# Gate products one tile of 128 outputs at a time, over the steps and the ends of all attention stages

## The reference

```python
# first block, per layer (D = 1024, 256 tokens)
h = rms_norm(x, mix_norm_g[l]);  proj = h @ w_in[l]
sb_q, sb_k, sb_v, sw_q, sw_k, sw_v, gate_logits = split(proj)     # gate_logits: 2 x 1024
y_sb  = stick_breaking_attention(sb_q, sb_k, sb_v) @ w_branch_sb[l]       # 8 heads of 64
y_swa = sliding_window_sink_attention(rope(norm(sw_q)), rope(norm(sw_k)), sw_v, sinks) @ w_branch_swa[l]
gates = sigmoid(gate_logits)
x = x + (gates[0] * y_sb + gates[1] * y_swa) @ w_out[l]
x = x + square(relu(rms_norm(x, mlp_norm_g[l]) @ w_up[l])) @ w_down[l]
# second block, per layer
x = layer_norm(a * x + 0.5 * swiglu(x))
#   token mixing: one w_in product, then four branches, each with a gate of 1024 outputs (4 x 1024):
#   ya gated MLP over tokens, yb short convolution, yc latent attention (MLA, 8 heads of 96),
#   yd sparse attention (compressed, selected and window keys, 8 heads of 64)
#   mix = (g0 * ya + g1 * yb + g2 * yc + g3 * yd) @ w_o[l]
x = layer_norm(a * x + mix);  x = layer_norm(a * x + cross_attention(x, mem))
x = layer_norm(a * x + 0.5 * swiglu(x))
```

## Time and profile before

| | us |
|---|---|
| median of 3 runs (2394.44 to 2394.92) | 2394.6 |
| the profiled execution | 2392.54 |
| its span, first to last instruction | 2390.8 |
| TensorE busy in the span | 2311.5 |
| VectorE busy | 1353.6 |
| ScalarE busy | 1152.1 |
| POOL busy | 186.9 |
| mean granted TensorE clock | 0.99 of full speed |
| read from memory | 392.9 MB, 165 GB/s over the span |

### The profile page before, as it was taken

How to read it: one execution, slowest core, us unless ns; L and a number is a source line. 1 busy time by engine, 2 the same in 40 slices (tenths; PEclk the granted TensorE clock), 3 DMA queues, 4 the chain that set the end, 5 groups by cost and what they waited for, 6 DMA issues and landing times.

```text
span 2390.8 us, 38487 instructions
## 1 busy us (share of the span) xinstructions
PE 2311.5 (97%) x16084; PEld 2123.2 (89%) x16098; DVE 1353.6 (57%) x1782; ACT 1152.1 (48%) x1797; POOL 186.9 (8%) x191
## 2 busy tenths in 40 slices
PE   7999999999999999999999999999999999998998
PEld 6988988888998998799998889989988999897997
DVE  4556555646664545655566665465555555776454
ACT  4754544674553444545443544454444445355443
POOL 0001210001110210000003001111100000110110
PEclk9999999999999999999999999999999999999999
DMA  6324555432555655554533545565555444263554
GB/s 223 132 97 152 184 197 181 163 121 97 190 189 185 222 182 189 171 181 141 168 106 110 190 156 181 191 208 188 187 174 184 155 158 143 80 205 134 184 178 146
DMA packets 109005, 395.93 MB, mean 166 GB/s; under 512 B 12374, under 2 KB 12544, under 8 KB 108576
## 3 DMA queue, kind: packets, MB, share of 16 engines
q1 hardware_dynamic: 104400, 377.53, 47.7%
q0 software_dynamic: 4432, 15.93, 2.2%
HBM read 392.92 MB, written 1.05 MB: 165 GB/s over the span
## 4 chain that ended last, share of the span: by engine, by line
PE 89%; DVE 5%; ACT 3%; DMA 1%; issue 1%; SPq 0%; DVEq 0%; ACTq 0%
PE psum L390 80%; PE psum L805 2%; PE psum L771 2%; DVE w_low L347 2%; PE psum L707 2%; DMA ring<-in_weights 1%; PE psum L789 1%; ACT w_high L344 1%; ACT attn_p L887 1%; PE psum L1773 1%; DVE mx L831 1%; DVE xT_low L666 0%; PE psum L1113 0%; ACT xT_high L660 0%; PE psum L1101 0%
## 5 line engine op out<-in xcount | busy, mean ns | idle before, releaser
L347 DVE TENSOR_TENSOR w_low<-ring,w_high 128x1024 fp32r<-128x1024 f32 x704 | 863.5, 1255 | 577.3 <-ACT w_high L344 575.7
L344 ACT ACTIVATE w_high<-ring 128x1024 fp32r<-128x1024 f32 x704 | 718.0, 1052 | 302.1 <-DMA ring<-in_weights 301.5
L390 PE MATMUL psum<-xT_high,w_high 128*128 128x256 f32 x2976 | 848.0, 285 | 0.0
L390 PE MATMUL psum<-xT_low,w_high 128*128 128x256 f32 x2976 | 843.3, 283 | 0.0
L390 PE MATMUL psum<-xT_high,w_low 128*128 128x256 f32 x2976 | 843.2, 283 | 0.0
L390 PEld LDWEIGHTS psum<-xT_high,w_high 128*128 128x128 f32 x2976 | 572.6, 192 | 0.8
L390 PEld LDWEIGHTS psum<-xT_low,w_high 128*128 128x128 f32 x2976 | 572.6, 192 | 0.4
L390 PEld LDWEIGHTS psum<-xT_high,w_low 128*128 128x128 f32 x2976 | 572.3, 192 | 0.0
L390 PE MATMUL psum<-w_high,hidden 128*128 128x512 f32 x1216 | 376.6, 390 | 0.0
L390 PEld LDWEIGHTS psum<-w_high,hidden 128*128 128x128 f32 x1216 | 228.3, 188 | 47.1
L390 PE MATMUL psum<-w_low,hidden 128*128 128x512 f32 x608 | 236.6, 389 | 0.0
(11 more groups left out here) (233 smaller groups left out, 2196.0 us busy)
## 6 DMA issues: line engine op xcount, KB each, us to landing
ring<-in_weights SPq DMA_DIRECT2D x706, 512.0 KB, 3.7
pages<-in_affine POOLq DMA_DIRECT2D x16, 512.0 KB, 5.6
ring<-in_weights SPq DMA_DIRECT2D x8, 440.0 KB, 3.3
pages<-in_gains POOLq DMA_DIRECT2D x4, 512.0 KB, 5.1
pages<-in_mem POOLq DMA_DIRECT2D x2, 1024.0 KB, 6.1
ring<-in_weights SPq DMA_DIRECT2D x4, 384.0 KB, 3.1
x<-in_x_in SPq DMA_DIRECT2D x2, 512.0 KB, 4.3
pages<-in_rows POOLq DMA_DIRECT2D x2, 512.0 KB, 6.2
```

The lines of the kernel that those rows point to most:

```text
L344: eng.activation(high, raw, ACT.Copy).then_inc(self.flag("w_rounded").sem, 1)
L347: eng.tensor_tensor(self.w_low[:, piece % SLOTS, 0:width], raw, high.bitcast(F32), ALU.subtract).then_inc(self.flag("w_split").sem, 1)
L390: m = pe.matmul(out, a, b, start=(first and i == 0), stop=(last and i == len(pairs) - 1))
```

## The change

Each gate tile of 128 outputs becomes a group of its own, 16 per layer in the first block and 32 in the second. It has its own bank (half filled), its own tanh of 128 x 256 and its own piece to split behind it; before, a group was two tiles, in the first block with one tanh of 128 x 512, in the second with two of 128 x 256. Matmuls, weight pieces and their bytes are the same. The tiles are distributed anew:

- first block: step 0 of the scan has tiles 0 and 1, steps 1 to 8 one each (2 to 9); 10 lies before the wait for the copied output, 11 before the turn of the keys; 12 beside step 1 and 13 beside step 6 of the sliding window, 14 behind its last values, 15 between the turn of its output and the wait for the parts;
- second block: 0 before the product `uq` and its wait for the turned latents; 1 and 2, 3 and 4, 5 and 6 where the groups 0, 1, 2 were; MLA's steps 0, 1, 2 and 6 have two each, 3, 4, 5 one; 18 behind MLA's values; 19 and 20, 21 and 22 around the compression; 23 to 31 beside steps 0 to 8 of the sparse attentions, then `ya` and `yb` at steps 9 to 16; `yc` 0 and 1 lie before the wait for the last output, 2 and 3 behind its turn.

The order of the weight pieces in memory, the counts of the semaphores and the bank order follow.

```diff
-GATES_PRE, GATES_MLA, GATES_NSA = 3, 10, 12
+GATES_SB = [[0, 1], [2], [3], [4], [5], [6], [7], [8], [9]]
+BESIDE_SWA = {0: [("ysb", 1)], 1: [("gate", 12)], 2: [("ysb", 2)], 4: [("ysb", 3)], 6: [("gate", 13)]}
+GATES_MLA = 19
+BESIDE_MLA = {0: [7, 8], 1: [9, 10], 2: [11, 12], 3: [13], 4: [14], 5: [15], 6: [16, 17]}
+BESIDE_NSA = dict(enumerate([("gate", n) for n in range(23, 32)] + [(y, n) for y in ("ya", "yb") for n in range(4)]))
...
@@ first block, TensorE
+            def gate(n):
+                c.gemm_features(pe, l, stream, banks, "gate", ("gate", n), xTf, KD, [("gate", n)])
...
                 if 1 <= h <= 8:
                     later_keys(h - 1)
-                if h < 8:
-                    c.gemm_features(pe, l, stream, banks, "gate", ("gate", h), xTf, KD,
-                                    [("gate", 2 * h), ("gate", 2 * h + 1)])
+                if h < 9:
+                    for n in GATES_SB[h]:
+                        gate(n)
                 if h >= 2:
                     sb_values(h - 2)
+            gate(10)
             pe.wait_ge(*c.flag("osb_ready").at(l, 2))
...
+            gate(11)
             c.wait_read_out(pe, l, "osb0", "osb1")
...
+            c.attend_tensor(pe, l, ("swa",), lambda i: [gate(n) if key == "gate" else branch_sb(n)
+                                                        for key, n in BESIDE_SWA.get(i, [])])
+            gate(14)
             pe.wait_ge(*c.flag("o_drained").at(l, 2))
...
+            gate(15)
             c.wait_read_out(pe, l, "osw0", "osw1")
@@ first block, ScalarE (VectorE splits the same pieces in the same places)
+            def gate(n):
+                act.activation(gates[:, n, :], c.filled(act, l, banks, ("gate", n))[:, 0:SEQ], ACT.Tanh, scale=0.5
+                               ).then_inc(*c.drained(banks, ("gate", n)))
+                after(("gate", n))
...
+            gate(14)
             for i in range(2):
                 c.part_out(act, l, "act", f"osw{i}", 4 + i, *(x[:, 2 * i:2 * i + 2, :] for x in oswT))
+            gate(15)
@@ second block, TensorE
+            c.gemm_features(pe, l, stream, banks, "gate", ("gate", 0), xT, KD, [("gate", 0)])
             c.wait_read_out(pe, l, "lat0", "lat1")
...
-            c.attend_tensor(pe, l, ("mla",), lambda i: group(BESIDE_MLA[i]) if i in BESIDE_MLA else None)
+            c.attend_tensor(pe, l, ("mla",), lambda i: gates(*BESIDE_MLA.get(i, [])))
+            gates(18)
...
             c.attend_tensor(pe, l, nsa, lambda i: group(BESIDE_NSA[i]) if i in BESIDE_NSA else None)
+            for n in range(2):
+                group(("yc", n))
             pe.wait_ge(*c.flag("o_drained").at(l, 8))
             turn_features("od", lambda k, t: o[:, t, k * P:(k + 1) * P])
-            group(("yc", 3))
+            for n in range(2, 4):
+                group(("yc", n))
             c.wait_read_out(pe, l, "od0", "od1")
```

More of the change, by code:

```diff
@@ L98, in stream_1, with gates, branch @@
     s.matrix("sbk", "w_in", D, span(512, 512), P, split=True)
-    s.matrix("gate", "w_in", D, span(2304, 2048), P, split=True)
-    s.matrix("ysb", "w_branch_sb", 512, span(0, D), P, split=True)
+    def gates(first, end):
+        for n in range(first, end):
+            for k in range(KD):
+                s.add(("gate", n, k), "w_in", k * P, span(2304 + n * P, P), split=True)
+    def branch(first, end):
+        for n in range(first, end):
+            for k in range(4):
+                s.add(("ysb", n, k), "w_branch_sb", k * P, span(n * P, P), split=True)
+    gates(0, 12)
+    branch(0, 4)
+    gates(12, 13)
+    branch(4, 8)
+    gates(13, 16)
     s.matrix("ysw", "w_branch_swa", 512, span(0, D), P, split=True)
@@ L121, in gates @@
             def gates(first, end):
-                for n in range(first, end):
-                    for tile in (2 * n, 2 * n + 1):
-                        for k in range(KD):
-                            s.add(("gate", tile, k), "w_in_2", k * P, span(4280 + tile * P, P), split=True)
+                for tile in range(first, end):
+                    for k in range(KD):
+                        s.add(("gate", tile, k), "w_in_2", k * P, span(4280 + tile * P, P), split=True)
+            gates(0, 1)
             s.matrix("uq", "mla_wuq_2", 256, span(0, 768), 384)
@@ L1001, in block_1 @@
             banks.add((key, t))
-    for key, n in (("sbq", 2), ("sbk", 2), ("gate", 8), ("ysb", 4), ("ysw", 4)):
-        for n in range(n):
+    for key, first, end in (("sbq", 0, 2), ("sbk", 0, 2), ("gate", 0, 12), ("ysb", 0, 2), ("gate", 12, 13), ("ysb", 2, 4),
+                            ("gate", 13, 16), ("ysw", 0, 4)):
+        for n in range(first, end):
             banks.add((key, n))
@@ L1048, in block_1 @@
     c.unit_list([window])
-    BESIDE = {0: 1, 2: 2, 4: 3}
     def added(t, n):
@@ L1401, in _ @@
                                          ).then_inc(*c.flag("sb_kept").one())
-                after(("gate", h))
+                for n in GATES_SB[h]:
+                    after(("gate", n))
                 next(side, None)
@@ L1405, in _ @@
                 pass
+            after(("gate", 9))
             c.settle(dve, l, "dve_step")
@@ L1409, in _ @@
                 dve.tensor_copy(osb[:, t, :], c.psum[:, 6 + t, :]).then_inc(*c.flag("osb_ready").one())
+            after(("gate", 10))
             for i in range(2):
@@ L1414, in _ @@
                             ).then_inc(*c.read_out("dve", "swq0"))
+            after(("gate", 11))
             c.turned(dve, l, "swk")
@@ L1564, in block_2 @@
             banks.add((key, t))
-    for key, n in (("gate", 16), ("ya", 4), ("yb", 4), ("yc", 4), ("yd", 4)):
-        for i in range(n):
+    for key, n in (("gate", 32), ("ya", 4), ("yb", 4), ("yc", 4), ("yd", 4)):
+        for i in range(1 if key == "gate" else 0, n):
             banks.add((key, i))
@@ L1994, in _ @@
             c.attend_scalar(act, l, nsa, beside_nsa)
+            for n in range(2):
+                after(("yc", n))
             for i in range(2):
                 c.part_out(act, l, "act", f"od{i}", 4 + i, *(x[:, 2 * i:2 * i + 2, :] for x in od_parts))
-            after(("yc", 3))
+            for n in range(2, 4):
+                after(("yc", n))
             for n in range(4):
```

138 lines of the change are left out of this document (74 added, 64 removed).

## The result

The kernel after takes **2357.7 us** (median of 5 runs, 2354.7 to 2359.1) against 2394.6 (5 runs beside them): ratio 0.984, 95% interval 0.9828 to 0.9853. The forecast was 2369.6 with a range from 2361 to 2383. Two more sets of runs of the same kernel gave 0.9851 and 0.9852 (E4, E11).

What follows compares the result with a forecast made beforehand. TensorE, busy 97% of the span, was taken as the bound, leaving its idle time and the clock to win. -2.6 + 8.7 + 13.3 - 3.1 + 12.7 = 29.0 us, less 4 = 25 us: 2369.6 us, range 2361 to 2383.

Steps and rivals of the forecast that it cites:

- part 5: Lower clock behind idle stretches that go: 12.7 us won, less 4 us set against it for two or three new stretches.
- part 4: MLA's steps: TensorE reaches the values of unit 2 early and waits for VectorE's finished output; 3.1 us lost in all.
- Part 1: First block's scan: ScalarE sets one-tile steps at 5.92 us and TensorE waits for its weights; 2.6 us lost.
- Part 2: First block's sliding-window attention: tiles cover the waits at unit 1 and at the end; 8.7 us won.
- part 3: Second block's seams: tiles and y products cover TensorE's idle time there; 13.3 us won in all.
- rival E: Whole kernel: none of the new stalls and no new stretch of lower clock; 2361 us, chance 0.08.
- B: Rival, four attention ends: gate work queued before the roundings eats the cover; 20 us back, 2390 us, chance 0.06.
- A: Rival, other one-tile steps: ScalarE's or VectorE's queue comes late there too; 11 us back, 2381 us, chance 0.12.
- C: Rival, short steps of scan, MLA and first sparse steps: lower clock once in each; slower, 2407 us, chance 0.05.
- D: Rival, scan steps: table switches cost the skill page's price, 3.2 us per step in 14 steps; 2409 us, chance 0.01.

Runs made afterwards that it cites:

- E4: The kernel after, unchanged, run again as the measure for other runs on its chip: 2358.2 us, ratio 0.9851 to the kernel before.
- E11: The kernel after, unchanged, run again on another chip with a further profiled execution: 2358.4 us, ratio 0.9852 to the kernel before.
- E8: The kernel after with weight-tile splits lagging one to three tiles in the scan, caught up at steps 8 to 11: 2359.7 us, 0.9849 of the kernel before.
- E10: The kernel after with a third logits bank and later splits, keys copied before the catching-up: 2348.5 us, 0.9807 of the kernel before.
- E5: The kernel after with tiles 13 to 15 moved beside sliding-window steps 3, 5 and 6, its end bare: 2369.5 us, 0.9892 of the kernel before.
- E6: The kernel after with gate tiles paired in the first four sparse steps, the sparse attentions' end bare: 2374.0 us, 0.9907 of the kernel before.
- E7: The kernel after, but in MLA's two-tile steps ScalarE waits for the second tile before the first tanh: 2357.3 us, 0.9848 of the kernel before.
- E2: Second block as in the kernel after, first block as in the kernel before: 2368.8 us, 0.9900 of the kernel before.
- E3: One-tile gate groups of the kernel after, but placed as in the kernel before, two per step: 2394.2 us, 1.0002 of the kernel before.
- E1: First block as in the kernel after, second block as in the kernel before: 2383.2 us, 0.9957 of the kernel before.
- E12: Three logits banks and later splits, with the gate tile issued before the later-keys matmuls in scan step 1: 2351.2 us, 0.9823 of the kernel before.
- E9: The kernel after with a third PSUM bank for the scan's logits: 2352.7 us, 0.9825 of the kernel before.

## Why the prediction was wrong

Two terms failed. The larger one is part 5, the clock, which was put at 8.7 us and measured 16.9. The other is part 4, a wait of 3.1 us that did not come.

**Part 1 (the scan, a loss of 2.6 us): right in its rows, wrong in its reason.** `logits` waits 1.22 us at step 2 of layer 0 (1.2 forecast), 0.36 in five steps (0.44), and in layer 1 it waits 1.55 instead of 3.2. There the lower clock, from 457.0 on, slowed step 1 of TensorE by 1.7 us while ScalarE was the one that was waited for, so it cost nothing and shortened the wait. Where the clock stayed up in this step, as in E11, the wait was near the 3.2 us of the forecast. The kernel after, then E11:

```profile
463.90 0.70 PE L1119 MATMUL psum<-pages 64*128 64x256 f32 x2 [1.55 <-ACT pages L1281]
...
463.31 1.22 PE L1119 MATMUL psum<-pages 64*128 64x256 f32 x2 [3.14 <-ACT pages L1281]
```

All `logits` waits sum to 6.4 us where I had 8.8. Of these 2.4 us, 1.7 stand in the busy time instead, so they gained nothing. E8 to E10 show that not ScalarE's queue (5.80 us) but the circle through the logits (5.91 us) set the steps.

**Part 2 (8.7 us) and part 3 (13.3 us): right.** Every row is gone or as small as forecast. Bare ends bring them back (E5: 6.2 us where 5.7 were expected; E6: 8.4 for 9.0).

**Part 4 (MLA, a loss of 3.1 us): wrong, the wait did not come.** I moved VectorE's finish 2.6 us earlier and it had to come 3.9 us earlier. The step of the sum that failed is "one w_high and one w_low less and the tanh sooner": I counted the work that leaves the queue, but not that ScalarE starts on the first of two tiles before the second is computed, in the two-tile steps before it, so that exponentials, maxima and copies all come earlier. The lower bound I had named, 0, was the true value, but by luck: I had given side work that slips forward as its reason. E7 takes the early tanh away and the wait returns with 1.05 us of the 1.35 forecast.

**Part 5 (the clock, 12.7 less 4 us): the term that was most mis-sized.** By busy time the clock gave 16.9 us. Ten stretches are gone, by an even share 1.7 us each. Nine stood at the covered places, about 15.3 us, where I had 12.7. Two more (1207.7 and 2170.2) are gone and one (457.0) is new, about 1.7 us less busy time where I had set 4 us of loss. Against the mean busy time of the three executions of after, 2297.0 us, the clock gave 14.5 us, so the size of this miss is itself uncertain by some 2 us. The covered places behaved as forecast, and more regularly than the one profile of before could show. Counted over the profiled executions of all kernels, by place and layer:

| place | lower clock where bare | where covered |
|---|---|---|
| sliding window, unit 1 and end (bare in before, E2, E3; the end alone in E5) | 14 of 14 | 0 of 42 |
| end of the sparse attentions (bare in before, E1, E3, E6) | 8 of 8, three in a row in 7 | 0 of 20 |
| behind the cross attention, bare in all | 7 of 8 where the sparse end is bare | 10 of 20 where it is covered |

The second row is where the one profile misled me: layer 1 had two stretches in that execution and three in every other, so I counted 2.3 us for it instead of 4.0. The third row is a place that I had left out, because nothing changes there: whether the clock falls behind the cross attention varies from execution to execution, and it fell less often when the sparse attentions before it ended without idle time. That this is caused by the change is not shown; 10 of 20 against 7 of 8 may be chance. The same is true of a fourth place, the small matmuls in the first steps of the sparse attentions (1207.7 in before, with no idle row in front): 5 of 6 with the second block of before, 10 of 22 with the new one. The 4 us set aside for new stretches had a cause. The first steps of the scan in layer 1 had one or two in every execution with the new scan except E10 and E12. At step 1 (as at 457.0) it lies in front of a wait for ScalarE and costs nothing. Behind the wait of 3.1 us at step 2 (E5, E7, E8, E11) it costs: E11 comes out of the block 2 us later than the other two executions of after.

The Trainium skill (TensorE: Matmul & The Clock Gate, HAM oscillation) describes idle time between groups of matmuls as what brings the lower clock back. The traces agree at the places of the first two rows: 22 of 22 bare, 0 of 62 covered. Its rule counts only longer gaps than these; here rows of 1.62 to 2.57 us were enough, and the measurement decides.

**The sum again.** Idle time: 16.3 forecast, 2.4 of waits that were smaller, 3.1 that did not come, 21.8, against 20.9 measured. Clock: 8.7 forecast, 16.9 measured. The range did not reach to the result for two reasons. I made the clock's term a single number with an allowance to one side only; a case in which further stretches of lower clock go was missing. And rival E, the edge of the range, was added up wrong: "none of the new stalls and no new stretch" takes back 8.8 + 3.1 + 4 us, which gives 2353.7 and not 2361. The 2361 is what comes out if only the ten waits of 0.44 us and the 4 us are taken back. Even so E is not what happened: its stalls of part 1 came. Among the chances, B at 2390 us is hardly below the limit of 4.8 us, so not most of its 0.06 but 0.01 of it is in the 0.89.

**The rivals.** A (more stalls in short steps): no, none beside the forecast ones. B (the cover is eaten): no, 0.19 us at the one end where I looked for 0.15, and none over 1 us. C (slower by the clock): refuted; 3 to 7 stretches in all, not 17 and more new ones. D (8.7 us per scan step by the Trainium skill's price of a table switch, ScalarE: Activation LUTs, What ACT_TABLE_LOAD costs): refuted by steps of 5.91 and 5.80 us with two loads of 1.28 us in each.

## What to carry to other kernels

Read the seams before the steps: where an engine at 97% still idles, independent work that is already being computed can be held back for the ends of stages. Finer pieces are easier to spread over many seams, but by themselves they bring nothing (E3). Before you relieve the engine that seems to set a step, look for a circle of about the same length through a shared buffer. Relieving the looser of the two limits gave nothing (E8), the tighter one some 3 to 5 us (E9), both 7 to 10 (E10). And treat the clock as a term with a spread: take it from several executions, place by place, and let the range reach to both sides.

## What the runs showed of the hardware

- The place counts as much as the length of the idle row. In the sliding window and at the sparse attentions' end, rows of 1.62 to 2.57 us were followed by 1.2 GHz in every execution that had them. The row of 1.45 us before the turn of `osb` was not, and behind the 2.59 us of the cross attention it varied. In step 1 of the scan the row of 1.86 to 1.88 us in layer 0 was followed by it in 12 of 13 executions, the row of 1.47 us in layer 1 in 5 of 13, and E12's row of 1.68 us there was not. What makes the difference stays open.
- The three profiled executions of the kernel after agree in TensorE's idle time within 2 us and differ in busy time by 6 us (2294.6, 2300.9 and 2295.5 us for after, E4, E11). So most of the 5.5 us between their spans is the clock.
- Two activations of ScalarE overlap by 0.1 us: in E9 the softplus starts at 93.95 us while the w_high lasts until 94.06. The tanh starts 0.1 us before the end of the weights' exponential too (92.74 against 92.35 + 0.49). The forecast counted the first overlap and not the second: its 5.92 us runs to the end of the exponential, and the step is 5.80.
